# The second norm's squares in two halves, filled blocks signalled one by one, both keys' places in one pass

## What is computed

```python
x  = x + gt1 * (concat(mla, mlstm) @ w_out)            # mixed x
h2 = rmsnorm(x, g_norm2) * (1 + sc2) + sh2             # the second norm
# peer(h2): 8 heads, 2 keys each, 128 keys a side, the best 16
q  = (h2 @ w_pq).reshape(128, 8, 2, 128)
s  = einsum('thpd,hpkd->thpk', q, sub_keys)
sv, si = top_k(s, 16)
cand = sv[.., 0, :, None] + sv[.., 1, None, :]         # 256 sums
cidx = si[.., 0, :, None] * 128 + si[.., 1, None, :]
best, pos = top_k(cand, 16);  eidx = take(cidx, pos)   # 16 experts a head
act = gelu(einsum('thkd,td->thk', expert_u[eidx], h2))
x   = x + gt2 * einsum('thk,thkd->td', softmax(best) * act, expert_v[eidx])
```

## Time and profile before

| | |
|---|---|
| three runs, median (lowest to highest) | 1372.97 us (1371.43 to 1375.32) |
| profiled execution, its own time | 1378.54 us |
| its span | 1377.1 us |
| busy: PE, DVE, ACT, POOL | 1031.6, 885.6, 475.3, 307.3 us |
| queue of the gathers (software_dynamic) | 268.45 MB |
| all DMA | 391.14 MB, mean 284 GB/s |
| mean granted TensorE clock | 0.866 |

### The profile page before, as it was taken

How to read it: one execution, slowest core, us unless ns; L and a number is a source line. 1 busy time by engine, 2 the same in 40 slices (tenths; PEclk the granted TensorE clock), 3 DMA queues, 4 the chain that set the end, 5 groups by cost and what they waited for, 6 DMA issues and landing times.

```text
span 1377.1 us, 17655 instructions
## 1 busy us (share of the span) xinstructions
PE 1031.6 (75%) x6291; PEld 590.1 (43%) x6291; DVE 885.6 (64%) x2281; ACT 475.3 (35%) x1312; POOL 307.3 (22%) x265
## 2 busy tenths in 40 slices
PE   7998999999899999999968787665434455443535
PEld 4776756577675647445534431332212222211201
DVE  5488643429864445845476798458866777777755
ACT  2013623101352521465347654333332233233321
POOL 0000000000000000000044444344435555443451
PEclk9999999999999999999989898876666666666667
DMA  8362453436237332145189999999999999999997
GB/s 305 132 223 92 160 214 130 183 105 249 93 131 281 117 104 93 62 183 203 55 358 426 409 426 427 425 412 368 426 426 426 426 426 426 427 426 426 427 426 306
DMA packets 56107, 391.14 MB, mean 284 GB/s; under 512 B 9931, under 2 KB 13055, under 8 KB 15955
## 3 DMA queue, kind: packets, MB, share of 16 engines
q0 software_dynamic: 37440, 268.45, 46.5%
q1 hardware_dynamic: 18578, 121.56, 23.9%
HBM read 387.89 MB, written 1.05 MB: 282 GB/s over the span
## 4 chain that ended last, share of the span: by engine, by line
DVE 21%; PE 16%; DMA 12%; ACT 5%; another core or an unknown queue 4%; issue 4%; POOL 1%; ACTq 0%; DVEq 0%
PE bank L169 16%; DMA e_uv<-in_experts_dram,e_listed 9%; DVE e_uv L2890 8%; DMA e_uv<-in_experts_dram,e_listed_uv 2%; DVE e_hot L185 1%; POOL e_uv L3095 1%; ACT e_diag L230 1%; DVE e_rest L2821 1%; ACT L230 1%; DVE e_e L210 1%; ACT m_W L230 1%; PE bank L174 1%; DMA m_w<-in_ada_dram 1%; DVE e_si L2825 1%
## 5 line engine op out<-in xcount | busy, mean ns | idle before, releaser
L3095 POOL DMA_INDIRECT e_uv<-in_experts_dram,e_listed x252 | 296.8, 1178 | 1035.3 <-DVE e_listed L202 806.9
L169 PE MATMUL bank<-e_uv,e_diag 128*32 128x512 f32 x1024 | 231.1, 879 | 285.0 <-ACT e_diag L230 254.5
L2890 DVE CUSTOM_DVE_ANT_0 e_uv<-e_uv,e_h2q 128x1024 f32<-128x1024 f32 x192 | 228.4, 1224 | 63.8 <-DMA e_uv<-in_experts_dram,e_listed 59.5
L169 PEld LDWEIGHTS bank<-e_uv,e_diag 128*32 128x32 f32 x1024 | 41.4, 140 | 409.7 <-ACT e_diag L230 283.5
L169 PE MATMUL bank<-hT,weights 128*128 128x256 f32 x640 | 141.0, 380 | 2.8 <-DVE hT L191 1.4
L169 PEld LDWEIGHTS bank<-hT,weights 128*128 128x128 f32 x640 | 120.8, 190 | 21.0 <-DVE hT L191 1.6
L230 ACT ACT_TABLE_LOAD x79 | 101.4, 1283 | 7.8 <-PE bank L169 1.7
L169 PE MATMUL bank<-weights,hT 128*128 128x512 f32 (+1 forms) x256 | 102.5, 557 | 1.7 <-DMA weights<-in_layer_q_dram 1.7
L197 DVE SCALAR_TENSOR_TENSOR conv<-ubuf,vec,conv 128x256 f32<-128x256 f32 x240 | 96.8, 480 | 0.6
L230 ACT ACTIVATE e_act<-e_dot 128x4 f32<-128x4 f32 (+1 forms) x81 | 16.6, 205 | 210.0 <-DVE e_dot L2890 200.7
L169 PE MATMUL bank<-weights,mixT 128*128 128x512 f32 x192 | 85.5, 598 | 2.4 <-DVE mixT L202 1.6
(11 more groups left out here) (385 smaller groups left out, 1429.5 us busy)
## 6 DMA issues: line engine op xcount, KB each, us to landing
weights<-in_ada_dram SPq DMA_DIRECT2D x8, 2048.0 KB, 8.7
weights<-in_layer_out_dram SPq DMA_DIRECT2D x6, 2048.0 KB, 8.1
e_w_pq<-in_w_pq_dram SPq DMA_DIRECT2D x12, 1024.0 KB
weights<-in_layer_cmp_dram SPq DMA_DIRECT2D x4, 2048.0 KB, 8.3
weights<-in_layer_q_dram SPq DMA_DIRECT2D x2, 2048.0 KB, 8.8
weights<-in_layer_kvc_dram SPq DMA_DIRECT2D x2, 2048.0 KB, 12.7
weights<-in_layer_gb_dram SPq DMA_DIRECT2D x2, 2048.0 KB, 15.1
weights<-in_layer_ga_dram SPq DMA_DIRECT2D x2, 2048.0 KB, 15.2
```

The source lines that it names most:

```text
L169: ins = self.engine.matmul(out, lhsT, rhs, start=start, stop=stop, **kw)
L2890: dve.mark(c.nc.vector.tensor_tensor_reduce(u, u, h2q[tt][n], 1.0, 0.0, MUL, ADD, m["dot"][:, j:j + 1]), ("dots_set", g, c0) if n == c1 - ...
L3095: ins = c.nc.gpsimd.indirect_dma_start(out=to, out_offset=None, in_=rows, in_offset=bass.IndirectOffsetOnAxis(ap=of, axis=0))
```

## The change

It has three parts. The norm: DVE now signals each mixed half, ACT squares each half by itself into totals of their own (columns 56+tt and 62+tt of `small`), the second not settled, and DVE adds the two. The fills: ACT's are no longer settled after the first, each block raises a semaphore, PE waits for each block by itself and takes them in the order 0, 4, 1, 5, 2, 6, 7, 3, for both halves of the key pair; the filling products of 512 and 256 columns ahead of `queries(0)` are gone, those of 256 ahead of the turned blocks stay. The places: both keys go through one set of operations twice as wide. Memory for that is found by letting `rest` lie in the first half of `hot`.

```diff
@@ Vector tile, mixed
-            c.dve.tt(self.x[:, tt, cols], self.x[:, tt, cols], xn[:, cols], ADD, tell=("x_mixed", tt) if h else None)
+            c.dve.tt(self.x[:, tt, cols], self.x[:, tt, cols], xn[:, cols], ADD, tell=("x_mixed", tt, h))
@@ Vector tile, mean_inverse
-        c.dve.wait_ge(*c.at("m_squares", "h2", tt))
-        mean_inverse(c.dve, small[:, 58 + tt:59 + tt], small[:, 56 + tt:57 + tt], D, ("m_inverse", "h2", tt))
+        mean = small[:, 58 + tt:59 + tt]
+        c.dve.wait_ge(*c.at("m_squares", "h2", tt, 0))
+        c.dve.ts(mean, small[:, 56 + tt:57 + tt], 1.0 / D, MUL, EPS, ADD)
+        c.dve.wait_ge(*c.at("m_squares", "h2", tt, 1))
+        c.dve.stt(mean, small[:, 62 + tt:63 + tt], 1.0 / D, mean, MUL, ADD)
+        c.dve.inverse(mean, mean, tell=("m_inverse", "h2", tt))
@@ Vector tile, filled
-                     m["mod"][:, 24 + kt, 0:1], ADD, tell=c.banks.emptied("h2T", tt, half) if k == 3 else None, settled=False)
+                     m["mod"][:, 24 + kt, 0:1], ADD,
+                     tell=c.banks.emptied("h2T", tt, half) if k == 3 else ("h2_filled_by_dve", tt, kt), settled=False)
@@ Scalar tile, squares
-        c.act.wait_ge(*c.at("x_mixed", tt))
-        c.act.f(self.s["sq"], self.x[:, tt, :], ACT.Square, accum_out=self.m["small"][:, 56 + tt:57 + tt], tell=("m_squares", "h2", tt))
+        for h, total in enumerate((56 + tt, 62 + tt)):
+            cols = slice(h * 512, h * 512 + 512)
+            c.act.wait_ge(*c.at("x_mixed", tt, h))
+            c.act.f(self.s["sq"][:, cols], self.x[:, tt, cols], ACT.Square, accum_out=self.m["small"][:, total:total + 1],
+                    settled=h == 0, tell=("m_squares", "h2", tt, h))
@@ Scalar tile, filled
-                    scale=m["scale2"][:, kt:kt + 1], bias=m["mod"][:, 24 + kt, 0:1],
-                    tell=c.banks.emptied("h2T", tt, half) if k == 3 else None)
+                    scale=m["scale2"][:, kt:kt + 1], bias=m["mod"][:, 24 + kt, 0:1], settled=k == 0,
+                    tell=c.banks.emptied("h2T", tt, half) if k == 3 else ("h2_filled_by_act", tt, kt))
@@ peer_tensor, queries
-            for kt in range(KT):
-                if k in (FIRST_OF[0], FIRST_OF[1]) and kt % 4 == 0:
-                    pe.wait_ge(*c.taken("h2T", tt, kt // 4))
+            for n, kt in enumerate((0, 4, 1, 5, 2, 6, 7, 3)):
+                if a == 0 and k in (FIRST_OF[0], FIRST_OF[1]):
+                    if kt % 4 == 3:
+                        pe.wait_ge(*c.taken("h2T", tt, kt // 4))
+                    elif tt == 0:
+                        pe.wait_ge(*at("h2_filled_by_dve" if kt >= 4 else "h2_filled_by_act", tt, kt))
+                    else:
+                        pe.wait_ge(*at("h2_filled_by_act", tt, kt))
...
@@ peer_tensor, the start
     first.normed_turned()
-    kept_busy(c, K, bank_q, 512, 256)
     queries(0)
@@ peer_vector, places
-        for a, (op, by) in enumerate(((ALU.logical_shift_right, 4), (ALU.bitwise_and, 15))):
-            dve.ts(part, pos, by, op)
-            dve.copy(partf, part)
-            dve.tt(hot, wide(partf.unsqueeze(2), shape), wide(K["iota"].unsqueeze(1), shape), ALU.is_equal)
-            dve.tt(hot, hot, wide(sif[:, a, :].unsqueeze(1), shape), MUL)
-            dve.total(e01[:, a], hot, ADD)
+        both = [P, 2, TOPK, TOPK]
+        dve.ts(part[:, 0], pos, 4, ALU.logical_shift_right)
+        dve.ts(part[:, 1], pos, 15, ALU.bitwise_and, settled=False)
+        dve.copy(partf, part)
+        dve.tt(hot, wide(partf.unsqueeze(3), both), wide(K["iota"].unsqueeze(1).unsqueeze(1), both), ALU.is_equal)
+        dve.tt(hot, hot, wide(sif.unsqueeze(2), both), MUL)
+        dve.total(e01, hot, ADD)
```

More of the change, by code:

```diff
@@ L91 @@
     "x_normed_by_dve": ("rms_inverse", "xn_ready", "block_inverse", "block_normed", "scale1_ready", "m_inverse",
-                        "x_mixed", "h2_normed", "x_scaled", "x_final"),
+                        "x_mixed", "h2_normed", "x_scaled", "x_final", "h2_filled_by_dve"),
     "lru_by_dve": ("lam_ready", "vec_halved", "lru_scale", "xc_ready", "lru_scanned", "lru_mixed"),
@@ L100 @@
                     "lstm_inverse", "lstm_gated"),
-    "x_normed_by_act": ("x_squares", "rms_ready", "block_squares", "block_root", "m_squares", "m_root"),
+    "x_normed_by_act": ("x_squares", "rms_ready", "block_squares", "block_root", "m_squares", "m_root", "h2_filled_by_act"),
     "lru_by_act": ("lam_exp", "lru_root", "zlru_tanh"),
@@ L1586, in second_memory @@
             ("keys", [P, 2, P], F32), ("keysT", [P, 2, P], F32), ("qT", [P, 2, P], F32), ("cand", [P, TOPK * TOPK], F32),
-            ("rest", [P, TOPK * TOPK], F32), ("hot", [P, TOPK, TOPK], F32), ("diag", [P, BUFS, SIDE], F32),
+            ("hot", [P, 2 * TOPK * TOPK], F32), ("diag", [P, BUFS, SIDE], F32),
             ("dot", [P, BUFS], F32), ("act", [P, BUFS], F32), ("spare", [P, 1], F32),
             ("listed", [P, 2, BUFS], U32), ("listed_uv", [P, 2, BATCH], U32), ("weight", [P, 2, BUFS], F32), ("sv", [P, 2, TOPK], F32), ("si", [P, 2, TOPK], U32),
-            ("sif", [P, 2, TOPK], F32), ("best", [P, 2, TOPK], F32), ("pos", [P, TOPK], U32), ("part", [P, TOPK], U32),
-            ("partf", [P, TOPK], F32), ("e01", [P, 2, TOPK], F32), ("gap", [P, TOPK], F32), ("norm", [P, 2], F32)):
+            ("sif", [P, 2, TOPK], F32), ("best", [P, 2, TOPK], F32), ("pos", [P, TOPK], U32), ("part", [P, 2, TOPK], U32),
+            ("partf", [P, 2, TOPK], F32), ("e01", [P, 2, TOPK], F32), ("gap", [P, TOPK], F32), ("norm", [P, 2], F32)):
         m[name] = tile(name, shape, dt)
+    m["rest"], m["hot"] = m["hot"][:, 0:TOPK * TOPK], m["hot"].rearrange("p (a i j) -> p a i j", a=2, i=TOPK)
     return m
@@ L1639, in mix_memory @@
     m["tmp"] = second["rest"][:, 0:6 * TILES * 8].rearrange("p (i t c) -> p i t c", i=6, t=TILES)
-    m["g_q"], m["g_k"] = second["cand"][:, 0:QK], second["hot"].rearrange("p i j -> p (i j)")[:, 0:QK]
+    m["g_q"], m["g_k"] = second["cand"][:, 0:QK], second["hot"][:, 1].rearrange("p i j -> p (i j)")[:, 0:QK]
     m["r1"], m["r2"] = (m["sides"].rearrange("p t a r -> p (t a r)")[:, i * 32 * MLA_H:(i + 1) * 32 * MLA_H]
@@ L2618, in queries @@
         for a in range(2):
-            for kt in range(KT):
-                if k in (FIRST_OF[0], FIRST_OF[1]) and kt % 4 == 0:
-                    pe.wait_ge(*c.taken("h2T", tt, kt // 4))
+            for n, kt in enumerate((0, 4, 1, 5, 2, 6, 7, 3)):
[6 more added lines that the diff above has]
+                        pe.wait_ge(*at("h2_filled_by_act", tt, kt))
                 pe.mm(bank_q[:, a * P:a * P + P], m["w_pq"][:, kt, a * P:a * P + P], hT[:, kt, tt * P:tt * P + P],
-                      start=kt == 0, stop=kt == KT - 1, tell=("queries_done", k) if (a, kt) == (1, KT - 1) else None)
+                      start=n == 0, stop=n == KT - 1, tell=("queries_done", k) if (a, n) == (1, KT - 1) else None)
     def scores(k):
```

## The result

The changed kernel took 1380.24 us (median of six, 1377.65 to 1381.29) against 1372.88 us (median of six, 1371.43 to 1375.32): ratio 1.0046, 95% interval 1.0035 to 1.0057, some 6.3 us slower (7.4 between the medians). The prediction was 1370.4 us. Its profiled execution took 1381.29 us.

What follows compares the result with a forecast made beforehand. The DMA queues were taken as saturated from about 700 us, with PE holding the first gather. Start 1.65 plus holes 0.95 gave 2.6 us off 1372.97, so 1370.4 us; range 1366.8 to 1374.6 us, counted as no change.

Steps and rivals of the forecast that it cites:

- the same 268 MB then pass at the same rate: Gathers behind the first: unchanged rate, so bringing the first gather forward counts in full; start's gain 1.65 us.
- a late list in more turns: Rival, chance 0.09: late gather lists in two further turns each cost a 3.2 us queue hole, ending at 1377.7 us.
- The prediction's own sign of being wrong: Wrong if the first gather moves and the end does not, or a new stretch under 0.95 DMA share appears.
- the 0.95 us that were put down to holes: Idle queues at 900 to 920 and 940 to 960 us: earlier lists gain 0.95 us in an ordinary run.
- Squares: Norm at the start: squaring the first half while DVE mixes the second gains 0.37 - 0.02 = 0.35 us.
- Fills and queries: First queries at the start: per-block waits end them at 4.55 instead of 5.88 us, gaining 1.33, taken as 1.3.
- PE's break at "issue": PE's list ahead of 684.76 us: a 1.33 us break no wait explains, kept at 1.3 us on both sides.
- Places: Key places in DVE's list: gain 0.77 us a turn, hidden in turn 0 and most later turns, counting at two holes.
- the holes of 900 and 940 us: Queue idle time of 0.4 and 3.2 us; earlier lists close 0.4 and 1.5 us, halved for an ordinary run.
- The size of the holes: Read from DMA shares 0.99 and 0.85 against 1.01: 0.4 and 3.2 us, half as large in an ordinary run.
- the clock rival: Rival, chance 0.08: without filling products PE's clock falls in the queries, costing 1.4 or 1.9 us, ending at 1372.2 us.
- the lower end of the range: Whole kernel: 1366.8 us, from the case in which the holes close, with the upper bound of the start.

## Why the prediction was wrong

- **The step that failed** is the last clause of the first paragraph on the bound: "the same 268 MB then pass at the same rate". I took the rate for a property of the queues, and costed `part` and `partf` by their operations only; that a tile of twice the size moves all later ones was there to be read in the change. The term was missing: 0.66% or 9.1 us (7.4 to 10.8) by the old kernel moved by 128 bytes, against a gain that I had at 2.6. No rival had it either; the one that ended slower (a late list in more turns, 1377.7 us) did not occur: there is no new hole like that of 940 us, only the 374 GB/s at 760 to 780 us. The prediction's own sign of being wrong came true: the first gather moved and the end did not.
- **The change's own worth** is a ratio of 0.9971, 4.0 us (2.5 to 5.5); forecast 2.6 on this scale. That 2.6 lies inside the interval is in part luck: the start gained 2.0 and not 1.65, the places alone 1.5 (0.1 to 3.0), and the 0.95 us that were put down to holes were mostly not there to be gained. With the address together: 1.0066 x 0.9971 = 1.0037, measured 1.0046 (1.0035 to 1.0057). The 1.2 us between them are within the intervals, and of the size of what the changed kernel lost at 760 to 780 us.
- **Squares.** 0.44 us (1.16 to 0.72) against 0.37. Right; a half from SBUF takes 0.63 us and not the 0.69 of the row that I took.
- **Fills and queries.** 1.35 us against 1.33: DVE's first fill and PE's own rate set them. The queries took 3.92 us instead of 3.81, which is the 0.1 us that PE waits for block 4 in the forecast's own count, so the eight waits cost nothing that shows. The first gather came 1.61 us sooner behind the first fill. PE's break at "issue" went from 1.33 us to 0.95 (ahead of 683.34 us) and made up 0.4 of it; I had held it equal. That part is luck: it was 1.18 to 1.53 us in the nine kernels with the old start and 0.95 to 1.22 in the five with the new one, and no run says what makes it.
- **Places.** Saved 0.91 us a turn, against 0.77, hidden in turn 0 as worked out. Their worth elsewhere was put in the wrong spot: the holes of 900 and 940 us come and go with the execution. The old kernel moved by 256 bytes has 1.01 in both stretches, with the old places. The kernel with the new places alone has a small hole (415 GB/s at 940 to 960 us). The loss that came back in every kernel before was at 760 to 780 us, where the share read 1.00 and only the 397 GB/s showed it.
- **The size of the holes.** I read it from the share. By the GB/s of the earlier trace rows against 426 they cost 20 x 23/426 = 1.1 and 20 x 88/426 = 4.1 us, not 0.4 and 3.2. Their 5.2 us are nearly all of the 5.6 by which the profiled execution lay above the median, so an ordinary run had hardly any of them, and not half.
- **The clock.** It did not fall: 1.00 from 669 to 675 us, the turned blocks and the queries included. The Trainium skill, "TensorE: Matmul & The Clock Gate", Part 4 (PE-mode transpose), has a transpose not count for the clock as a product does; no drop here bears that out or rules it out.
- **From the sum.** The whole miss of 9.8 us is the missing term (9.1) less what the change gained beyond the forecast (1.4), with 2.1 us left over: 1.1 between the medians' difference (7.4) and the ratio's (6.3), and the 1.2 us named above, less rounding. Three figures of the working were off too, none of which matters: the lower end of the range is 1367.3 by its own terms (1372.97 - 3.6 - 2.1) and not 1366.8, the clock rival's sum is 1372.0 and not 1372.2, and a turn's gathers take 39.4 us at the 426 GB/s of the long stretch and not 40.3.

## What to carry to other kernels

When a kernel is bound by its queues, GB/s over a long saturated stretch is the number to compare, and not the share. Every edit that changes the size of a tile moves the ones behind it: look at the start of the DMA targets modulo 256 in both builds before anything is put down to an edit's instructions, and keep the targets of saturated transfers at a multiple of 256 by padding. (Here it paid for the gathers; aligning the weight loads gained nothing that could be told.) A change that is worth 4 us looked like a loss of 6 through 128 bytes.

## What the runs showed of the hardware

Indirect gathers of rows of 8 KB into SBUF ran at 426 GB/s where each partition's target started at a multiple of 256 bytes, at 421 at 64 or 128 bytes off and at 419 at 32 bytes off, with the DMA share at 1.01 in each case. At 128 bytes off it was 421 too when DVE's and PE's busy time was about half (102 of 211 and 75 of 133 us).

The Trainium skill, "DMA: Bandwidth & Descriptors", section "How a descriptor splits into AXI transactions", says that a descriptor is split into transactions of 256 bytes, and that one which starts off a multiple of 256 begins with a read from the boundary below, whose unused bytes cost too. It says so of reads; here the sources stayed and the target moved. By its count an 8 KB row needs 33 transactions instead of 32, an estimate of 3%, or 260, 258 and 257 beats of 32 bytes instead of 256 at 128, 64 and 32 bytes off, an estimate of 1.6, 0.8 and 0.4%. The direction agrees and so does the grain of 256 bytes. The sizes don't: the measured rate fell by 1.2, 1.2 and 1.6%, most where the page's beats would have it least.
